# A two-layer fused block on one core: the sum of squares of the recurrence's heads as two rounded products, four key tiles later

## The chip, the cores and the metric

The kernel runs on one core of a Trainium2 chip. It is one program for a network of several layers. The metric is its device time in microseconds (us); the median of three runs of the kernel before is 1331.39 us.

## The reference

A sequence of 512 tokens with 1024 channels passes through three layers, in float32: a gated MLP with a spatial mix, a chunked attention, and a second block that has two branches. This case is about the first branch of the second block, a gated linear recurrence with 8 heads of 128 channels:

```python
def hgrn2_branch(hq, hf, hi, hz, lb, hg_norm_g):
    f = lb + (1.0 - lb) * jax.nn.sigmoid(hf.astype(jnp.float32))
    q = jax.nn.silu(hq.astype(jnp.float32)).reshape(B, S, HG_HEADS, HG_DIM)
    k = (1.0 - f).reshape(B, S, HG_HEADS, HG_DIM)
    v = hi.astype(jnp.float32).reshape(B, S, HG_HEADS, HG_DIM)
    log_f = jnp.log(f).reshape(B, S, HG_HEADS, HG_DIM)
    o = hgrn2_recurrence(q, k, v, log_f).astype(dt)
    o = rms_norm_2(o, hg_norm_g)
    o = o * jax.nn.silu(hz).reshape(B, S, HG_HEADS, HG_DIM)
    return o.reshape(B, S, HG_WIDTH)

def rms_norm_2(x, g):
    xf = x.astype(jnp.float32)
    y = xf * lax.rsqrt(jnp.mean(xf * xf, axis=-1, keepdims=True) + EPS)
    return (y * g.astype(jnp.float32)).astype(x.dtype)
```

`hgrn2_recurrence` computes S_t = diag(f_t) S_{t-1} + k_t v_t^T and o_t = S_t^T q_t in chunks. hq, hf, hi, hz and mz are slices of one projection of the normalised input. The mean of `rms_norm_2` over a head's 128 channels is what the change touches.

## The kernel before

Channels lie on the 128 partitions and the 512 tokens along the free dimension, so one head is a tile of 128 x 512. Weights come in slabs of 128 x 1024 (8 key tiles of 128 x 128). SyncE (SP) issues a slab's transfer into `raw`. ScalarE (ACT) rounds it to `whi` (line 1048, wherever its program says `cut()`), a type of fewer bits called fp32r. GpSimd (POOL) subtracts, and the rest is `wlo` (line 479). Every large product is then three products of rounded operands, hi x hi, hi x lo and lo x hi (lines 489 to 491, `mm3`), which TensorE (PE) takes faster than one of full float32. A ring of four slabs lies between ACT and PE.

Each engine has its own program, and works it in the order in which it is written; semaphores join the engines. A name such as `hoA.at("ln", u)` means ACT's step "ln" of head u. In the recurrence the rounds r = 0 to 8 overlap three heads: PE computes the projections of head r and the recurrence of head s = r - 1, and the normalisation of head u = r - 2 is finished.

PE's round is: slab hq of head r into bank 1, with pieces of the scores between its key tiles (`hg_scores`: the product of the squared output after key tile 2, the turned keys after 3, diagonal blocks after 4 and 5, cross blocks 0 and 1 after 6, 2 and 3 after 7); slab hf into bank 0, with the state's updates after key tiles 3 to 5 (`hg_updates`, which wait for the keys' low part, line 1830 on DVE); slab mz of head s into bank 7, after the masked copies (line 1840, step "far"); slab hz into bank 2, with the outputs (`hg_outputs`) into bank 3. The cross products of blocks 0 and 1 are written to bank 6, those of 2 and 3 to bank 7. Therefore `hg_cross` waits, at block 2, for the Silu of mz of head s - 1, which reads bank 7:

```python
                if t == 2 and s >= 1:
                    pe.wait_ge(mzA.sem, mzA.at("z", s - 1))
```

After round 7 the slabs dn 0 to 5 take the places of the next head's slabs.

ACT's round r is: `hg_root(u)` (the Square of the output in bank 3, line 1263; after PE's product the logarithm from bank 6, line 1265, and the exponential, line 1267); a slab's rounding; `hg_silu_z` of head s (line 1273, with a table load); `ml_silu_z(r - 2)` (the Silu of mz, line 1277); `hg_keys` (line 1283); a rounding; `hg_scores`; then the Silu of hq, the sigmoid and the logarithm of the forget gate and the decays of head r, and `hg_halves` (the rounded copies, lines 1325 to 1331).

VectorE (DVE) does in round r: `hg_finish(u)` (lines 1819 to 1826: norm, gate, and the two halves of y), `hg_stage(s)` (lines 1830 to 1851), `hg_project(r)` (lines 1856 to 1903; its last four subtractions are the low halves, line 1896 klo, 1898 kolo, 1900 qlo and 1903 qblo).

The product itself is `hg_square` on PE (line 762), in full float32: a matrix of ones with `ho[:, 0, :]` gives every partition the sum over the channels. It waits for the Square and for "far" of head u, and writes bank 6; cross block 0 of the next head waits for the logarithm, which reads that bank.

Of the kernel before, what the change touches and what calls it, by code (L numbers as in the profile page):

```python
# [22 lines left out]
F32 = mybir.dt.float32  # L23
F32R = mybir.dt.float32r
U32 = mybir.dt.uint32
ALU = mybir.AluOpType
ACT = mybir.ActivationFunctionType

P = 128
S = 512  # L30
# [8 lines left out]
HH = 8  # L39
# [105 lines left out]
def build(nc, xt, w, vecs, ws, bs, relx, consts, masks_hg, masks_ml, xs, rel_tab, tk, out):  # L145
    ctx = ExitStack()
    with ctx:
        def sb(name, shape, dt, where=ctx):
            return where.enter_context(nc.sbuf_tensor(name, shape, dt))
# [76 lines left out]
        with ExitStack() as scope:  # L226
            he = sb("he", [P, S], F32, scope)
            hf = sb("hf", [P, S], F32, scope)
            hk = sb("hk", [P, S], F32, scope)
            hb = sb("hb", [P, S], F32, scope)  # L230
            hd = sb("hd", [P, S], F32, scope)
            heb = sb("heb", [P, S], F32, scope)
            hen = sb("hen", [P, S], F32, scope)
            hq = sb("hq", [P, S], F32, scope)
            hx = sb("hx", [P, TT, 12], F32, scope)
            hfac = sb("hfac", [P, TT, 12], F32, scope)
            hqx = sb("hqx", [P, TT, HX], F32, scope)
            hqxs = [sb(n, [P, TT, HX], F32R, scope) for n in ("hqxhi", "hqxlo")]
            hqb = sb("hqb", [P, TT - 1, P], F32, scope)
            hqbs = [sb(n, [P, 2, TT - 1, P], F32R, scope) for n in ("hqbhi", "hqblo")]  # L240
            hks = [sb(n, [P, S], F32R, scope) for n in ("hkhi", "hklo")]
            hkos = [sb(n, [P, S], F32R, scope) for n in ("hkohi", "hkolo")]
            hkb = sb("hkb", [P, TT - 1, P], F32, scope)
            hkts = [sb(n, [P, TT - 1, P], F32R, scope) for n in ("hkthi", "hktlo")]
            hs = sb("hs", [P, S], F32, scope)
            hss = [sb(n, [P, S], F32R, scope) for n in ("hshi", "hslo")]
            hst = sb("hst", [P, TT - 1, P], F32, scope)
            hsts = [sb(n, [P, TT - 1, P], F32R, scope) for n in ("hsthi", "hstlo")]
            hz = sb("hz", [P, 2, S], F32, scope)
            ho = sb("ho", [P, 2, S], F32, scope)  # L250
            hm = sb("hm", [P, S + P + CROSS], F32, scope)
# [54 lines left out]
        def steps(name, names, rounds=1, prime=0):  # L306
            s = Steps(sem(name), names, rounds, prime)
            all_steps.append(s)
            return s
# [58 lines left out]
        htA = steps("ht_act", ["z", "kthi", "shi", "sthi"], HH)  # L368
        htV = steps("ht_dve", ["ktlo", "diag", "near", "mid", "far", "slo", "st1", "st2", "st3", "stlo"], HH)
        hoP = steps("ho_pe", ["ms"], HH)  # L370
        hoA = steps("ho_act", ["sq", "ln", "root"], HH)
        hoV = steps("ho_dve", ["norm", "y", "yhi", "ylo"], HH)
        mzA = steps("mz_act", ["z"], HH)
        hzV = steps("hz_dve", ["zero", "one0", "one1"])
        dnP = steps("dn_pe", ["tok", "wide"])
        dnA = steps("dn_act", numbered("sq", QL + KL) + ["kp", "root", "wide0", "wide1"] + numbered("hi", QL + KL))
        dnV = steps("dn_dve", ["q1", "q2", "k1"] + ["turn"] + numbered("cross", 4) + ["sum", "mean", "inv", "kplo", "diag"]
# [38 lines left out]

        def col(name, i=0):
            return vec[:, bass.ds(VEC[name] + i, 1)]

        def f32(ap):  # L420
            return ap.bitcast(F32)
# [62 lines left out]
        def _(pe):  # L484
# [261 lines left out]
            def hg_cross(s, t):  # L746
                if t == 0:
                    if s >= 1:
                        pe.wait_ge(htV.sem, htV.at("far", s - 1))
                        pe.wait_ge(hoA.sem, hoA.at("ln", s - 1))  # L750
                if t == 2 and s >= 1:
                    pe.wait_ge(mzA.sem, mzA.at("z", s - 1))
                cols = slice(t * P, (t + 1) * P)
                last = mm3(banks[:, 6 * S + t * 2 * P:6 * S + t * 2 * P + CROSS], [u[:, cols] for u in hkos],
                           [u[:, t, HC:HX] for u in hqxs], True, True)
                if t == TT - 1:
                    last.then_inc(htP.did("cross"), 1)

            def hg_square(u):
                pe.wait_ge(hoA.sem, hoA.at("sq", u))  # L760
                pe.wait_ge(htV.sem, htV.at("far", u))
                nc.tensor.matmul(bank[6], ones, ho[:, 0, :], start=True, stop=True).then_inc(hoP.did("ms"), 1)  # L762

            def hg_scores(r, k):
                s, u = r - 1, r - 2
                if k == 2 and u >= 0:
                    hg_square(u)
                if k == 3:
                    hg_keys(s)
                if k in (4, 5):  # L770
                    hg_diagonal(s, 2 * (k - 4))
                    hg_diagonal(s, 2 * (k - 4) + 1)
                if k in (6, 7):
                    hg_cross(s, 2 * (k - 6))
                    hg_cross(s, 2 * (k - 6) + 1)

            def hg_updates(s, k):
# [29 lines left out]
            for r in range(HH):  # L807
                s = r - 1
                scores, updates, outputs = (lambda k: hg_scores(r, k), lambda k: hg_updates(s, k),
                                            lambda k: hg_outputs(s, k))  # L810
                if s < 0:
                    scores = updates = outputs = None
                if r >= 1:
                    pe.wait_ge(hpA.sem, hpA.at("q", r - 1))
                if r == 1:
                    pe.wait_ge(hvV.sem, hvV.all())
                slab("hq", r, bank[1], h, between=scores, tiles=n2V if r == 0 else None)
                if r >= 1:
                    pe.wait_ge(hpA.sem, hpA.at("f", r - 1))
                slab("hf", r, bank[0], h, between=updates)  # L820
                if s >= 0:
                    pe.wait_ge(htV.sem, htV.at("far", s))
                    slab("mz", s, bank[7], h)
                if r == 0:
                    values(1)
                if r == 0:
                    pe.wait_ge(n2V.sem, n2V.all())
                if r >= 1:
                    pe.wait_ge(htA.sem, htA.at("z", s))
                slab("hz", r, bank[2], h, between=outputs)  # L830
# [2 lines left out]
            pe.wait_ge(hpA.sem, hpA.at("q", s))  # L833
            slab("dn", 0, bank[1], h, between=lambda k: hg_scores(HH, k))
            pe.wait_ge(hpA.sem, hpA.at("f", s))
            slab("dn", 1, bank[0], h, between=lambda k: hg_updates(s, k))
            pe.wait_ge(htV.sem, htV.at("far", s))
            slab("mz", s, bank[7], h)
# [191 lines left out]
        def _(act):  # L1030
# [228 lines left out]
            def hg_root(u):  # L1259
                if u >= 1:  # L1260
                    act.wait_ge(hoV.sem, hoV.at("ylo", u - 1))
                act.wait_ge(htP.sem, htP.at("o", u))
                nc.scalar.activation(ho[:, 0, :], bank[3], ACT.Square).then_inc(hoA.did("sq"), 1)
                act.wait_ge(hoP.sem, hoP.at("ms", u))
                nc.scalar.activation(ho[:, 1, :], bank[6], ACT.Ln, bias=eps, scale=1.0 / P).then_inc(hoA.did("ln"), 1)
                act.wait_ge(hoA.sem, hoA.at("ln", u))
                nc.scalar.activation(ho[:, 1, :], ho[:, 1, :], ACT.Exp, scale=-0.5).then_inc(hoA.did("root"), 1)

# [228 lines left out]
        def _(dve):  # L1497
# [316 lines left out]
            def spread(ap, shape):  # L1814
                return ap.to_broadcast([P, *shape])

            def hg_finish(u):
                dve.wait_ge(hoA.sem, hoA.at("root", u))
                V.scalar_tensor_tensor(ho[:, 0, :], bank[3], cols("hg_g", 1)[0], ho[:, 1, :], ALU.mult,
                                       ALU.mult).then_inc(hoV.did("norm"), 1)  # L1820
                dve.wait_ge(hoV.sem, hoV.at("norm", u))
                V.tensor_tensor(ho[:, 0, :], ho[:, 0, :], hz[:, u % 2, :], ALU.mult).then_inc(hoV.did("y"), 1)
                dve.wait_ge(hoV.sem, hoV.at("y", u))
                V.tensor_copy(yhi[:, u, :], ho[:, 0, :]).then_inc(hoV.did("yhi"), 1)
                dve.wait_ge(hoV.sem, hoV.at("yhi", u))
                V.tensor_tensor(ylo[:, u, :], ho[:, 0, :], f32(yhi[:, u, :]), ALU.subtract).then_inc(hoV.did("ylo"), 1)
# [27 lines left out]
            def hg_project(r):  # L1854
# [44 lines left out]
                dve.wait_ge(hpA.sem, hpA.at("qhi", r))  # L1899
                V.tensor_tensor(hqxs[1][:, :, :], hqx[:, :, :], f32(hqxs[0][:, :, :]),  # L1900
                                ALU.subtract).then_inc(hpV.did("qlo"), 1)
                dve.wait_ge(hpA.sem, hpA.at("qbhi", r))
                V.tensor_tensor(hqbs[1][:, r % 2, :, :], hqb[:, :, :], f32(hqbs[0][:, r % 2, :, :]),
                                ALU.subtract).then_inc(hpV.did("qblo"), 1)
# [1 line left out]
            V.memset(hs[:, :], 0.0).then_inc(hzV.did("zero"), 1)  # L1906
            V.memset(hfac[:, :, 0:1], 1.0).then_inc(hzV.did("one0"), 1)
            V.memset(hfac[:, :, 11:12], 1.0).then_inc(hzV.did("one1"), 1)
            dve.wait_ge(st_x, 16)
            dve.wait_ge(ld_hm, 16)  # L1910
            dve.wait_ge(hzV.sem, hzV.all())
# [300 lines left out]
```

## Time and profile before

| | |
|---|---|
| median of three runs | 1331.39 us (1330.42 to 1332.16) |
| the profiled execution | 1331.94 us |
| its span in the trace | 1330.0 us |
| mean granted clock of PE | 0.994 of full speed |
| PE busy | 1299.5 us |
| DVE, ACT, POOL busy | 730.7, 663.1, 495.9 us |

The page sums up one profiled execution. Times are us unless marked ns. "PEld" is PE's weight load, which overlaps the matmuls. The timeline's rows give the start, the duration, the engine, the line and the tiles; a bracket at the end holds the idle time before the instruction and what ended it. Matmuls are pipelined: the next one starts before the last has ended, so the distance between starts, not the duration, is what each takes from the stream. The product of ones has two records per head.

### The profile page before, as it was taken

What the parts mean: (1) busy time and instruction counts of PE and PEld (TensorE: products, weight loads), DVE (VectorE), ACT (ScalarE), POOL (GpSimd) and SP (SyncE); (2) the same over time, 40 slices, a digit from 0 to 9 for tenths busy, and PEclk for the clock granted to TensorE, in tenths of its full rate; (3) what the DMA queues carried; (4) which work ended last, traced back from release to release, by engine and by line L of the source; (5) the groups of instructions that cost most, each with busy time, mean ns of one, the idle gap of its engine ahead of it and who ended that gap; (6) DMA issues with size and microseconds to landing.
All of it is one profiled execution on the core that took longest, in us unless ns stands there. A gap on an engine that the chain in (4) does not pass through costs nothing.

```text
span 1330.0 us, 16592 instructions
## 1 busy us (share of the span) xinstructions
PE 1299.5 (98%) x6492; PEld 1086.2 (82%) x6492; DVE 730.7 (55%) x1290; ACT 663.1 (50%) x998; POOL 495.9 (37%) x206
## 2 busy tenths in 40 slices
PE   6999999999999999999999999999999999999997
PEld 4788888888887788888887888888878888888897
DVE  6473655643129256565766377676646556642454
ACT  4344454443335566666446566665536555552321
POOL 3453443344434332322336433333333233344520
PEclk9999999999999999999999999999999999999998
DMA  6543233234333232231243322222223222335411
GB/s 227 177 140 98 89 94 95 90 101 142 95 111 89 86 109 79 93 95 63 65 158 93 110 80 64 64 78 72 73 88 99 72 90 72 97 93 177 145 54 64
DMA packets 43309, 132.33 MB, mean 99 GB/s; under 512 B 7072, under 2 KB 11872, under 8 KB 42592
## 3 DMA queue, kind: packets, MB, share of 16 engines
q1 hardware_dynamic: 37856, 116.41, 28.1%
q10 hardware_dynamic: 5376, 14.87, 3.2%
q8 instruction: 51, 0.84, 0.3%
q14 instruction: 26, 0.21, 0.1%
HBM read 124.97 MB, written 10.49 MB: 102 GB/s over the span
## 4 chain that ended last, share of the span: by engine, by line
PE 80%; DVE 10%; ACT 6%; issue 2%; POOL 1%; DMA 0%; DVEq 0%; SPq 0%; ACTq 0%
PE banks L489 24%; PE banks L491 24%; PE banks L490 24%; PE banks L656 2%; DVE hd L1862 1%; PE banks L648 1%; PE banks L637 1%; DVE naccb L1767 1%; DVE ylo L1664 1%; ACT L1307 1%; ACT L1306 1%; PE banks L881 1%; PE banks L762 1%; DVE nfull L1660 1%; DVE hb L1859 1%
## 5 line engine op out<-in xcount | busy, mean ns | idle before, releaser
L479 POOL TENSOR_TENSOR wlo<-raw,whi 128x1024 fp32r<-128x1024 f32 (+2 forms) x198 | 486.2, 2457 | 761.2 <-ACT whi L1048 760.9
L489 PE MATMUL banks<-hhi,whi 128*128 128x512 f32 x752 | 304.7, 405 | 2.1 <-DVE hlo L1794 1.2
L1048 ACT ACTIVATE whi<-raw 128x1024 fp32r<-128x1024 f32 (+2 forms) x198 | 205.9, 1041 | 176.6 <-PE banks L491 104.5
L491 PE MATMUL banks<-hlo,whi 128*128 128x512 f32 x752 | 293.8, 391 | 0.0
L490 PE MATMUL banks<-hhi,wlo 128*128 128x512 f32 x752 | 293.4, 390 | 0.0
L489 PE MATMUL banks<-yhi,whi 128*128 128x512 f32 x448 | 176.6, 394 | 0.2 <-DVE ylo L1664 0.2
L491 PE MATMUL banks<-ylo,whi 128*128 128x512 f32 x448 | 174.7, 390 | 0.0
L490 PE MATMUL banks<-yhi,wlo 128*128 128x512 f32 x448 | 174.4, 389 | 0.0
L489 PEld LDWEIGHTS banks<-hhi,whi 128*128 128x128 f32 x752 | 141.6, 188 | 31.7 <-issue 2.8
L491 PEld LDWEIGHTS banks<-hlo,whi 128*128 128x128 f32 x752 | 141.1, 188 | 30.3
L490 PEld LDWEIGHTS banks<-hhi,wlo 128*128 128x128 f32 x752 | 141.7, 188 | 26.9 <-issue 2.2
L489 PE MATMUL banks<-whi,yhi 128*128 128x512 f32 x224 | 91.6, 409 | 15.3 <-DVE ylo L1523 12.3
L489 PEld LDWEIGHTS banks<-yhi,whi 128*128 128x128 f32 x448 | 84.1, 188 | 21.3 <-issue 3.0
L491 PEld LDWEIGHTS banks<-ylo,whi 128*128 128x128 f32 x448 | 84.1, 188 | 18.0
L490 PEld LDWEIGHTS banks<-yhi,wlo 128*128 128x128 f32 x448 | 84.2, 188 | 17.0
L490 PE MATMUL banks<-whi,ylo 128*128 128x512 f32 x224 | 89.4, 399 | 0.0
L491 PE MATMUL banks<-wlo,yhi 128*128 128x512 f32 x224 | 89.4, 399 | 0.0
L489 PEld LDWEIGHTS banks<-whi,yhi 128*128 128x128 f32 x224 | 43.5, 194 | 26.3 <-POOL wlo L479 15.7
L490 PEld LDWEIGHTS banks<-whi,ylo 128*128 128x128 f32 x224 | 43.6, 195 | 9.7 <-issue 0.7
L491 PEld LDWEIGHTS banks<-wlo,yhi 128*128 128x128 f32 x224 | 43.3, 193 | 9.4
L1610 DVE SCALAR_TENSOR_TENSOR mt<-banks,vec,bb 128x512 f32<-128x512 f32 x16 | 12.0, 751 | 68.3 <-PE banks L578 68.3
L1179 ACT ACTIVATE sc<-sc,sm 128x128 f32<-128x128 f32 (+1 forms) x64 | 35.1, 550 | 27.5 <-DVE sm L1722 27.5
(382 smaller groups left out, 2198.7 us busy)
## 6 DMA issues: line engine op xcount, KB each, us to landing
raw<-w SPq DMA_DIRECT2D x194, 512.0 KB, 3.6
rel_tab<-relx ACTq DMA_DIRECT2D x1, 4096.0 KB, 20.1
tab<-rel_tab SPq DMA_DIRECT2D x16, 224.0 KB, 3.5
x<-xt SPq DMA_DIRECT2D x4, 512.0 KB, 6.6
x<-xt ACTq DMA_DIRECT2D x1, 2048.0 KB, 9.4
x_kept<-x ACTq DMA_DIRECT2D x1, 2048.0 KB, 7.5
parts_kept<-mcg SPq DMA_DIRECT2D x8, 256.0 KB, 4.3
mgt<-parts_kept SPq DMA_DIRECT2D x8, 256.0 KB, 4.1
```

Source lines behind the costliest of these rows:

```text
L479: nc.gpsimd.tensor_tensor(lo[:, 0:width], raw[:, n % 2, 0:width], f32(hi[:, 0:width]), ALU.subtract).then_inc(lo_done, 1)
L489: nc.tensor.matmul(dst, a[0], b[0], start=first, stop=False)
L490: nc.tensor.matmul(dst, a[1], b[0], start=False, stop=False)
L491: return nc.tensor.matmul(dst, a[0], b[1], start=False, stop=last)
L637: done = nc.tensor.matmul(banks[:, c:c + QW[t]], a[rows, t * P:(t + 1) * P], b[rows, 0:QW[t]], start=first, stop=last)
L648: last = nc.tensor.transpose(banks[:, c:c + P], sc[:, q, of:of + P], ident)
L656: last = nc.tensor.matmul(bank[AO[i][q]][:, k * P:S], av[q][:, i, k, :], p[:, q, AK[q][k]:AK[q][k] + KW[k]], start=k == 0 and p is phi, st ...
L762: nc.tensor.matmul(bank[6], ones, ho[:, 0, :], start=True, stop=True).then_inc(hoP.did("ms"), 1)
L881: last = nc.tensor.transpose(bank[b][:, c:c + P], msc[:, QO[t] + k * P:QO[t] + (k + 1) * P], ident)
L1048: nc.scalar.activation(parts(slab)[0][:, 0:width], raw[:, n % 2, 0:width], ACT.Copy).then_inc(hi_done, 1)
L1179: e = nc.scalar.activation(row, row, ACT.Exp, bias=sm[:, q, 1, t:t + 1], accum_out=sm[:, q, 2, t:t + 1])
L1306: nc.scalar.activation(he[:, :], bank[0], ACT.Sigmoid).then_inc(hpA.did("f"), 1)
```

## The change

In the recurrence the product of ones with the squared output of head u becomes two products of rounded operands. ACT makes a rounded copy `hsqhi` of the square behind the Square, once DVE has read `hq` (whose place it shares); DVE subtracts it into `hsqlo` (which shares the place of `heb`), between qlo and qblo of the next head, or in `hg_finish` for the last head. A rounded copy of the ones, `hones`, is made once. PE issues the two products in key tile 6 of slab hq, after cross block 0, instead of after key tile 2. For heads 0 to 6 they are written to bank 0, which slab hf fills next, so slab hf waits for the logarithm; for the last head to bank 6, as before, and behind slab dn 3, as before. The wait of cross block 0 for the logarithm is gone.

```diff
+            hsqlo = sb("hsqlo", [P, S], F32R, scope)
+            hsqhi = sb("hsqhi", [P, S], F32R, scope)
+            hones = sb("hones", [P, P], F32R, scope)
...
+        def sum_bank(u):
+            return bank[0] if u < HH - 1 else bank[6]
...
                 if t == 0:
                     if s >= 1:
                         pe.wait_ge(htV.sem, htV.at("far", s - 1))
-                        pe.wait_ge(hoA.sem, hoA.at("ln", s - 1))
                 if t == 2 and s >= 1:
                     pe.wait_ge(mzA.sem, mzA.at("z", s - 1))
...
             def hg_square(u):
-                pe.wait_ge(hoA.sem, hoA.at("sq", u))
-                pe.wait_ge(htV.sem, htV.at("far", u))
-                nc.tensor.matmul(bank[6], ones, ho[:, 0, :], start=True, stop=True).then_inc(hoP.did("ms"), 1)
+                pe.wait_ge(hoV.sem, hoV.at("sqlo", u))
+                if u < HH - 1:
+                    pe.wait_ge(hpA.sem, hpA.at("f", u + 1))
+                else:
+                    pe.wait_ge(htV.sem, htV.at("far", u))
+                nc.tensor.matmul(sum_bank(u), hones[:, :], hsqhi[:, :], start=True, stop=False)
+                nc.tensor.matmul(sum_bank(u), hones[:, :], hsqlo[:, :], start=False, stop=True).then_inc(hoP.did("ms"), 1)
 
             def hg_scores(r, k):
                 s, u = r - 1, r - 2
-                if k == 2 and u >= 0:
-                    hg_square(u)
...
                 if k in (6, 7):
                     hg_cross(s, 2 * (k - 6))
+                    if k == 6 and u >= 0:
+                        hg_square(u)
                     hg_cross(s, 2 * (k - 6) + 1)
...
+                if r >= 2:
+                    pe.wait_ge(hoA.sem, hoA.at("ln", r - 2))
                 slab("hf", r, bank[0], h, between=updates)
...
+            pe.wait_ge(hoA.sem, hoA.at("ln", s - 1))
             slab("dn", 1, bank[0], h, between=lambda k: hg_updates(s, k))
...
                 nc.scalar.activation(ho[:, 0, :], bank[3], ACT.Square).then_inc(hoA.did("sq"), 1)
+                act.wait_ge(hoA.sem, hoA.at("sq", u))
+                act.wait_ge(hpV.sem, hpV.at("qin", min(u + 1, HH - 1)))
+                nc.scalar.activation(hsqhi[:, :], ho[:, 0, :], ACT.Copy).then_inc(hoA.did("sqhi"), 1)
                 act.wait_ge(hoP.sem, hoP.at("ms", u))
-                nc.scalar.activation(ho[:, 1, :], bank[6], ACT.Ln, bias=eps, scale=1.0 / P).then_inc(hoA.did("ln"), 1)
+                nc.scalar.activation(ho[:, 1, :], sum_bank(u), ACT.Ln, bias=eps, scale=1.0 / P).then_inc(hoA.did("ln"), 1)
...
+            def hg_square(u):
+                dve.wait_ge(hoA.sem, hoA.at("sqhi", u))
+                V.tensor_tensor(hsqlo[:, :], ho[:, 0, :], f32(hsqhi[:, :]), ALU.subtract).then_inc(hoV.did("sqlo"), 1)
...
             def hg_finish(u):
+                if u == HH - 1:
+                    hg_square(u)
...
+                if r >= 1:
+                    hg_square(r - 1)
                 dve.wait_ge(hpA.sem, hpA.at("qbhi", r))
...
+            V.tensor_copy(hones[:, :], ones).then_inc(hzV.did("ones"), 1)
```

## Rows read from the trace of the kernel before

**Rows 1.** The page, part 1: busy time, share, instructions.
```profile
PE 1299.5 (98%) x6492; PEld 1086.2 (82%) x6492; DVE 730.7 (55%) x1290; ACT 663.1 (50%) x998; POOL 495.9 (37%) x206
```

**Rows 2.** Windows view, 30 us of the recurrence; the columns stand in the row.
```profile
core 0: us, PE busy (x) PEld busy (x) DVE busy (x) ACT busy (x) POOL busy (x), PEclk, DMA share, GB/s
790.00:820.00 30.00, 29.85 (x159) 24.95 (x158) 20.59 (x36) 19.04 (x27) 10.87 (x4) 1.00 0.24 74
```

**Rows 3.** Waits from 720 to 1000 us: us in total, times, longest.
```profile
PEld banks L762 <- ACT ho L1263: 4.0, 7, 0.6
...
ACT ho L1265 <- PE banks L762: 12.9, 8, 4.4
```

**Rows 4.** Timeline, PE around the product of head 0: start us, us.
```profile
769.74 0.39 PE L491 MATMUL banks<-hlo,whi 128*128 128x512 f32 x1
...
770.26 0.30 PEld L762 LDWEIGHTS banks<-ho,cst 128*128 128x128 f32 x2 [0.55 <-ACT ho L1263]
770.26 1.12 PE L762 MATMUL banks<-ho,cst 128*128 128x512 f32 x2
...
771.45 0.39 PE L490 MATMUL banks<-hhi,wlo 128*128 128x512 f32 x1
...
771.68 0.39 PE L491 MATMUL banks<-hlo,whi 128*128 128x512 f32 x1
...
772.71 0.19 PEld L489 LDWEIGHTS banks<-hqxhi,hkhi 128*128 128x128 f32 x1
...
799.88 0.70 PE L762 MATMUL banks<-ho,cst 128*128 128x512 f32 x1 [0.15 <-ACT ho L1263]
```

**Rows 5.** Timeline, ACT from the Square to the Silu of mz.
```profile
769.63 0.58 ACT L1263 ACTIVATE ho<-banks 128x512 f32<-128x512 f32 x1
771.43 0.69 ACT L1265 ACTIVATE ho<-banks,cst 128x512 f32<-128x512 f32 x1 [1.22 <-PE banks L762]
...
772.68 1.04 ACT L1048 ACTIVATE whi<-raw 128x1024 fp32r<-128x1024 f32 x1
773.75 1.28 ACT L1273 ACT_TABLE_LOAD   x1
775.04 0.60 ACT L1273 ACTIVATE hz<-banks 128x512 f32<-128x512 f32 x1
775.53 0.59 ACT L1277 ACTIVATE mzg<-banks 128x512 f32<-128x512 f32 x1
```

**Rows 6.** Timeline, PE: cross block 1, end of key tile 7, cross block 2.
```profile
775.98 0.27 PE L489 MATMUL banks<-hqxhi,hkohi 128*128 128x192 f32 x1
...
776.80 0.39 PE L491 MATMUL banks<-hlo,whi 128*128 128x512 f32 x1
...
777.03 0.25 PE L489 MATMUL banks<-hqxhi,hkohi 128*128 128x192 f32 x1
```

**Rows 7.** Timeline, DVE: low halves, the keys' low part, the masked copies.
```profile
769.09 0.68 DVE L1896 TENSOR_TENSOR hklo<-hen,hkhi 128x512 fp32r<-128x512 f32 x1
...
770.29 1.08 DVE L1900 TENSOR_TENSOR hqxlo<-hqx,hqxhi 128x896 fp32r<-128x896 f32 x1
...
777.47 0.55 DVE L1830 TENSOR_TENSOR hktlo<-banks,hkthi 128x384 fp32r<-128x384 f32 x1
...
778.77 1.43 DVE L1840 COPY_PREDICATED hs<-hm,banks 128x384 f32<-128x384 uint32 x3
```

**Rows 8.** Timeline, PE: first state update, first matmul of slab mz.
```profile
780.45 0.22 PE L489 MATMUL banks<-yhi,hkthi 128*128 128x128 f32 x1
...
784.21 0.39 PE L489 MATMUL banks<-hhi,whi 128*128 128x512 f32 x1
```

**Rows 9.** Timeline and windows view around the longest later pause of PE.
```profile
45.19 0.77 PE L489 MATMUL banks<-whi,yhi 128*128 128x512 f32 x1 [3.00 <-POOL wlo L479]
...
48.72 0.39 PE L491 MATMUL banks<-wlo,yhi 128*128 128x512 f32 x1
...
46.00:47.00 1.00, 1.00 (x3) 0.75 (x3) 0.00 (x0) 0.00 (x0) 1.00 (x1) 0.50 0.95 152
```

More of the change, by code:

```diff
@@ L231, in build @@
             hd = sb("hd", [P, S], F32, scope)
-            heb = sb("heb", [P, S], F32, scope)
+            with ExitStack() as place:
+                heb = sb("heb", [P, S], F32, place)
+            hsqlo = sb("hsqlo", [P, S], F32R, scope)
             hen = sb("hen", [P, S], F32, scope)
-            hq = sb("hq", [P, S], F32, scope)
+            with ExitStack() as place:
+                hq = sb("hq", [P, S], F32, place)
+            hsqhi = sb("hsqhi", [P, S], F32R, scope)
+            hones = sb("hones", [P, P], F32R, scope)
             hx = sb("hx", [P, TT, 12], F32, scope)
@@ L370, in build @@
         hoP = steps("ho_pe", ["ms"], HH)
-        hoA = steps("ho_act", ["sq", "ln", "root"], HH)
-        hoV = steps("ho_dve", ["norm", "y", "yhi", "ylo"], HH)
+        hoA = steps("ho_act", ["sq", "sqhi", "ln", "root"], HH)
+        hoV = steps("ho_dve", ["sqlo", "norm", "y", "yhi", "ylo"], HH)
         mzA = steps("mz_act", ["z"], HH)
-        hzV = steps("hz_dve", ["zero", "one0", "one1"])
+        hzV = steps("hz_dve", ["zero", "one0", "one1", "ones"])
         dnP = steps("dn_pe", ["tok", "wide"])
```

## The prediction

> **What bounds the kernel now.** I read the page first: TensorE (PE) has work in 98% of the span [rows 1]. In a stretch of 30 us in the middle of the recurrence it is busy 29.85 us, at a granted clock of 1.00, while VectorE (DVE) is busy 20.59, ScalarE (ACT) 19.04 and GpSimd (POOL) 10.87 us [rows 2]. So what is added to PE's stream, or makes it stand still, lengthens the kernel one for one, and work on the other engines is free until PE waits for it. The waits of this stretch come next: PE waits for the squared output seven times, 4.0 us in sum, at the place that the change touches, and ACT waits 12.9 us for the product that follows [rows 3]. ACT's idle time costs nothing by itself. I then laid one round of the timelines side by side (the product of head 0 at 770.26 us) and asked of every instruction behind the moved product who waits for it. The rounds repeat: the same instructions stand 29.6 us later each time (line 762 again at 799.88) [rows 4].
>
> **The product itself.** Before it, line 491 begins at 769.74 us; a pair of 512-column products follows each other by 0.23 us (771.45 to 771.68). Without the product line 490 of key tile 3 would have begun at 769.74 + 2 x 0.23 = 770.20; it begins at 771.45 [rows 4]. So wait and float32 product together cost PE 1.25 us: 770.26 - 769.97 = 0.29 of waiting for the Square, 0.96 of product. The two rounded products are of the same form as the stream around them and cost 2 x 0.23 = 0.46 us. The Square's output is 2.7 us old or more at the new place, so the first wait goes. Gain on PE: 1.25 - 0.46 = 0.79 us a round, seven times. For the last head the product stays where it is, behind slab dn 3, and only its kind changes: 0.96 - 0.46 = 0.5 us gained, once.
>
> **The added instructions.** ACT gets one rounding copy a round, of 128 x 512 like the Square of 0.58 us, between Square and logarithm [rows 5]; ACT waits there for the product anyhow. It is done by about 770.9 (769.63 + 2 x 0.6). DVE gets one subtraction, 0.68 us by the row of the same form; it stands behind the subtraction of line 1900, which ends at 771.37, so it is ready at about 772.1 [rows 7]. The new product comes at 774.7 (below): 2.6 us of cover, so neither costs anything. Line 1903, now 0.7 us later, is wanted only in slab hz, over 20 us later. The copy of the ones is made once, before the loop, 128 columns wide, beside a PE that has other work: nothing. The wait for the forget gate's sigmoid before bank 0 is written concerns an instruction of the round before: nothing. PE runs 1.25 us earlier in key tiles 3 to 6, and its weight load for the diagonal products moves from 772.71 to 771.46 [rows 4], against line 1900's end at 771.37 [rows 7]: 0.04 us are left after the 0.05 that a signal takes. I put this at zero, at most 0.1 us a round.
>
> **What the move delays.** This is the term that decides. The product was issued after key tile 2 and is now issued in key tile 6, between the cross products of block 0 and block 1. That place is 775.98 us before [rows 6], so 775.98 - 1.25 = 774.73 in the changed kernel. The second of the two begins at 774.96, lasts 0.39 like its neighbours [rows 4], and ends at 775.35; ACT starts 0.05 us later, as it did behind the old one (770.26 + 1.12 = 771.38, then 771.43) [rows 4, 5]. The logarithm so begins at 775.40 instead of 771.43: 3.97 us later.
>
> ACT works its list strictly in order, and behind the logarithm stand, without an idle moment between them: the exponential, a slab's rounding (line 1048), a table load of 1.28 us, the Silu of hz and the Silu of mz, which ends at 775.53 + 0.59 = 776.12 [rows 5]. All of them move by 3.97 us: the Silu of mz ends at 780.09. PE waits for exactly this one: hg_cross of block 2, in key tile 7, waits for mzA "z" of the head before, because blocks 2 and 3 are written to bank 7, which that Silu reads. Before the change the wait was met, since the matmul of block 2 began at 777.03 [rows 6] and the Silu had ended 0.9 us earlier. Now the square that is issued in key tile 6 releases a chain of 4.7 us on ACT, and the wait at its end comes some 1.1 us of PE work later. With 0.05 us for the signal and a weight load of 0.19 the matmul of block 2 begins at 780.33. Without the wait it would begin at 777.03 - 0.79 = 776.24. PE stands still for 4.1 us, and the round ends 780.33 - 777.03 = 3.30 us later than before. Heads 0 to 6 have this round, the last head has not: 7 x 3.30 = 23.1 us.
>
> What is late next? DVE's chain hangs on the exponential too: the low part of the keys (line 1830) ends at 778.02 and would end at 781.99 [rows 7]; the update that needs it stood at 780.45 and stands at 783.75 after the stall [rows 8]. The masked copies end at 780.20, so at 784.17 [rows 7], for slab mz, which moves from 784.21 to 787.51 [rows 8]. Both are covered by the stall itself. The new wait of slab hf for the logarithm (ending at 776.1) is covered too. The slabs' rounding moves with ACT, but its results are wanted a slab or more later, and POOL is busy a third of the time. SP's transfers start from POOL's end and move by the same 4 us, beneath that lead.
>
> **The clock.** PE's last matmul before the stall (line 491, 776.80 [rows 6]) would start at 776.01 and end at 776.40, so PE is idle for 3.9 us. The trace has one comparable pause: 3.00 us idle before 45.19. Behind it the granted clock is 0.50, the level of 1.2 GHz, and the eight matmuls from 45.19 to 48.72 took 3.53 us instead of 8 x 0.23 = 1.84: 1.7 us lost [rows 9]. So each of the seven stalls can cost between nothing and 1.7 us on top. I take 1.2: the pause is longer than the one that cost 1.7, but when the clock falls while PE still stands, a part of the slow time runs out unused. That makes 7 x 1.2 = 8.4 us, between 0 and 12.
>
> The Trainium skill, "TensorE: Matmul & The Clock Gate", section "Why this matters for your kernels", warns of idle gaps between matmul bursts, which bring the clock back to half rate. By that rule each stall pays the term, by its absence the stalls cost 23.1 us alone; the pause of 3.00 us in this trace agrees with the page.
>
> **Sum.** Profiled span 1330.0 + 23.1 - 0.5 + 8.4 = 1361.0 us. The profiled execution took 1331.94, 1.94 around its span, and stands 0.55 over the median of 1331.39. So 1361.0 + 1.94 - 0.55 = 1362.4 us.
>
> **Rivals.**
> - No loss of clock: the stall is as computed, and PE returns at full clock. 1362.4 - 8.4 = 1354.0. For it: the trace holds one such pause, in another stage and beside other work. Against it: rows 9, a shorter pause that did cost. Chance 0.14.
> - Full loss of clock in every round, 12.0 us: 1366.0. For it: the pause is longer than that of rows 9. Chance 0.13.
> - The Silu of mz isn't what PE meets, and the keys' low part is: the update would stand at 780.45 - 0.79 = 779.66 and find its operand at 781.99, a stall of 2.3 us, 1.5 net, a pause short of that of rows 9. 7 x 1.5 - 0.5 = 10.0: 1341.4. Against it: the order of ACT's list and the wait in hg_cross are both in the code. Chance 0.04.
> - The other side: the chain on ACT ends in time. The mechanism is the slack at block 2 in key tile 7: the wait costs nothing as long as logarithm to Silu of mz fits into the 0.9 us that PE needs from the product's end to that matmul, and it decides from there. Then only the gain of PE remains: 7 x 0.79 + 0.5 = 6.0, 1325.4. The chain is 4.69 us long in rows 5, table load and slab's rounding included, and would have to be four fifths shorter. Chance 0.04 for this result, 0.01 for a chain so nearly hidden that gain and stall cancel.
>
> **How the numbers follow.** The forecast has 0.64. The range 1353 to 1368 takes in the first two rivals and the bounds of the clock term, and leaves out those with 0.09. A difference under 0.2% (2.7 us) couldn't be told from no change. Faster: 0.04; same: 0.01; slower: 0.95, the sum of the forecast, both clock cases and the keys.
>
> **What would show it.** In the profile of the changed kernel: two fp32r matmuls on the square between 192-column cross products, seven times, and no wait of PE on line 1263's output in them; seven waits of PE's weight load on the Silu of mz, about 3.9 us each, some 27 in sum, a wait that isn't there before; ACT's wait for the product near 4.5 us a round instead of 1.2; heads 32.9 us or more apart instead of 29.6; a granted clock under 1.00 in stretches of the recurrence; no wait on the keys' low part or on the masked copies. The prediction is wrong if PE doesn't wait at block 2, or waits without the clock falling (then by 8 us), or if the two rounded products cost far from 0.46 us.

## The result and the profile after

The changed kernel takes 1368.28 us (median of four runs, 1366.86 to 1369.89) against 1331.78 us for the kernel before in the same comparison: a ratio of 1.0273, 95% interval 1.0257 to 1.0290. It is slower by 36.5 us; forecast were 31.0, and the time lies 0.3 us above the upper end of the range.

The profiled execution took 1368.03 us, its span is 1366.1 us and the mean granted clock 0.982 of full speed (before: 1330.0 us and 0.994). The page's part 1 and the head of part 2 of the changed kernel, beside [rows 1]:

```profile
span 1366.1 us, 16610 instructions
PE 1310.0 (96%) x6492; PEld 1097.2 (80%) x6492; DVE 737.3 (54%) x1299; ACT 667.4 (49%) x1006; POOL 494.4 (36%) x206
...
PE   6999999999999999999999888888899999999997
```

PE is 10.5 us longer busy, although the changed products take less of its stream (part of its matmuls last longer, see below), and it stands still for longer as well: seven of the forty slices, those of the recurrence, fall from 9 to 8. The waits view of 720 to 1036 us says on whom (engine and line that waited, who ended it, us in sum, times, longest), beside [rows 3]:

```profile
PE banks L497 <- ACT mzg L1294: 26.3, 7, 3.8
...
PEld banks L497 <- ACT mzg L1294: 29.3, 7, 4.2
...
ACT ho L1282 <- PE banks L773: 35.0, 8, 4.5
```

Line 497 is the first of the three products of `mm3` in the new file, 1294 the Silu of mz, 773 the second rounded product, 1282 the logarithm. No wait of PE on the Square is left, and there is no other new one. The timeline of the first such round, beside [rows 5, 6]:

```profile
768.91 0.58 ACT L1277 ACTIVATE ho<-banks 128x512 f32<-128x512 f32 x1
...
773.98 0.42 PE L772 MATMUL banks<-hsqhi,hones 128*128 128x512 f32 x1
774.24 0.39 PE L773 MATMUL banks<-hsqlo,hones 128*128 128x512 f32 x1
...
774.67 0.69 ACT L1282 ACTIVATE ho<-banks,cst 128x512 f32<-128x512 f32 x1 [4.51 <-PE banks L773]
775.39 0.63 ACT L1284 ACTIVATE ho<-ho 128x512 f32<-128x512 f32 x1
775.93 1.04 ACT L1062 ACTIVATE whi<-raw 128x1024 fp32r<-128x1024 f32 x1
776.99 1.28 ACT L1290 ACT_TABLE_LOAD   x1
778.28 0.60 ACT L1290 ACTIVATE hz<-banks 128x512 f32<-128x512 f32 x1
778.77 0.59 ACT L1294 ACTIVATE mzg<-banks 128x512 f32<-128x512 f32 x1
...
775.27 0.40 PE L499 MATMUL banks<-hlo,whi 128*128 128x512 f32 x1
779.42 0.53 PE L497 MATMUL banks<-hqxhi,hkohi 128*128 128x192 f32 x1 [3.75 <-ACT mzg L1294]
...
781.72 0.63 PE L499 MATMUL banks<-hlo,whi 128*128 128x512 f32 x1
...
784.69 0.40 PE L497 MATMUL banks<-hhi,whi 128*128 128x512 f32 x1
```

The rows show the Square (768.91), the chain without a gap from the product to the Silu of mz (774.24 to 779.36), PE's cross block 2 starting 0.06 us behind it, and what follows: a matmul of 512 columns lasts 0.63 us instead of 0.39 until 784.7. The windows view gives the clock in these stretches (last columns: granted clock, DMA share, GB/s):

```profile
776.00:779.00 3.00, 0.00 (x0) 0.00 (x0) 2.88 (x3) 2.97 (x5) 1.96 (x1) 0.80 0.00 0
779.00:780.00 1.00, 0.58 (x3) 0.58 (x3) 1.00 (x1) 1.00 (x3) 0.73 (x1) 0.50 0.00 0
780.00:784.00 4.00, 4.00 (x13) 3.32 (x13) 3.17 (x7) 1.27 (x3) 2.38 (x1) 0.50 0.49 137
785.00:790.00 5.00, 5.00 (x28) 4.29 (x27) 0.99 (x3) 0.59 (x1) 0.00 (x0) 1.00 0.19 78
```

In this round the clock falls to half, 1.2 GHz, while PE stands still, and is back at 2.4 GHz at 784.7, when PE has worked for 5.2 us. Not every round is like this. Read in windows of 0.2 us, the clock is at half from 777.8 to 784.7, 815.4 to 818.8, 849.5 to 852.9, 883.6 to 887.1, 917.8 to 921.2, 951.9 to 958.7 and 989.5 to 992.9 us, while PE starts again at 779.42, 814.68, 849.08, 883.52, 917.95, 952.25 and 988.09. In four of the seven rounds it therefore falls only after PE has started again, and in the first and the sixth it stays low for 6.8 us instead of 3.4. The third and the sixth round:

```profile
849.10:849.50 0.40, 0.40 (x3) 0.40 (x4) 0.40 (x1) 0.40 (x2) 0.30 (x1) 1.00 0.00 0
849.60:852.80 3.20, 3.20 (x11) 2.62 (x11) 3.00 (x7) 0.76 (x1) 2.36 (x1) 0.50 0.48 164
...
952.00:958.60 6.60, 6.34 (x18) 5.28 (x19) 4.71 (x8) 2.64 (x5) 2.95 (x2) 0.50 0.51 144
```

The sum of the seven rounds can be read from the Squares on ACT. They lie 35.25, 34.42, 34.43, 34.43, 34.31, 35.83 and 32.88 us apart; before they lay 29.61, 29.60, 29.62, 29.61, 29.67, 29.65 and 28.10 us apart. That is 35.7 us in all. Block 2 comes 779.42 - 768.91 = 10.51 us behind the Square and came 777.03 - 769.63 = 7.40 behind it: 3.11 us a round (the other rounds agree within 0.02), 21.8 in sum, are the wait, less PE's gain. The rest, 2.53, 1.71, 1.70, 1.71, 1.53, 3.07 and 1.67 us, 13.9 in sum, is the half clock. The intervals above give nearly the same: half of the low time in which PE works is 2.6, 1.7, 1.7, 1.7, 1.6, 3.2 and 1.7 us, 14.3 in sum.

### The profile page after: what moved, and what is told of

The parts are those of the page before. It is cut to its first block, busy times and chain, and to the rows that moved or that the text cites. A ratio compares the mean times of both kernels' runs of the same rounds, so it can differ in the third digit from the quotient of the medians.

```text
span 1366.1 us, 16610 instructions
## 1 busy us (share of the span) xinstructions
PE 1310.0 (96%) x6492; PEld 1097.2 (80%) x6492; DVE 737.3 (54%) x1299; ACT 667.4 (49%) x1006; POOL 494.4 (36%) x206
## 4 chain that ended last, share of the span: by engine, by line
PE 86%; DVE 6%; ACT 4%; issue 2%; POOL 1%; DMA 1%; DVEq 0%; SPq 0%; ACTq 0%
PE banks L497 27%; PE banks L499 26%; PE banks L498 26%; PE banks L664 1%; PE banks L656 1%; PE banks L645 1%; DVE naccb L1784 1%; DVE ylo L1681 1%; ACT whi L1062 1%; DMA raw<-w 1%; ACT L1290 1%; PE banks L895 1%; DVE nfull L1677 1%; PE banks L586 1%; DVE hlo L1811 0%
## 5 line engine op out<-in xcount | busy, mean ns | idle before, releaser
L498 PE MATMUL banks<-hhi,wlo 128*128 128x512 f32 x752 | 298.1, 396 | 0.0
L499 PE MATMUL banks<-hlo,whi 128*128 128x512 f32 x752 | 297.9, 396 | 0.0
L497 PEld LDWEIGHTS banks<-hhi,whi 128*128 128x128 f32 x752 | 144.8, 193 | 31.3 <-DVE hlo L1811 2.8
L499 PEld LDWEIGHTS banks<-hlo,whi 128*128 128x128 f32 x752 | 144.2, 192 | 31.4
L498 PEld LDWEIGHTS banks<-hhi,wlo 128*128 128x128 f32 x752 | 144.9, 193 | 26.3 <-issue 0.2
## 6 DMA issues: line engine op xcount, KB each, us to landing
rel_tab<-relx ACTq DMA_DIRECT2D x1, 4096.0 KB, 20.4
```

The source lines that it names most:

```text
L497: nc.tensor.matmul(dst, a[0], b[0], start=first, stop=False)
L498: nc.tensor.matmul(dst, a[1], b[0], start=False, stop=False)
L499: return nc.tensor.matmul(dst, a[0], b[1], start=False, stop=last)
```

## The experiments

Each was measured in three rounds with the kernel before on the same chip. The first three take the changed kernel's mechanism apart, the next two its halves, the last five look for an order in which the change pays.

**Another place: after key tile 4.** 

```diff
-                    if k == 6 and u >= 0:
+                    if k == 4 and u >= 0:
                         hg_square(u)
```

(The call stands behind the second diagonal block of that tile.)

> The changed kernel with the two products after key tile 4 instead of 6, 2.4 us earlier. Theory: the chain to the Silu of mz starts 2.4 us earlier, so a round loses 3.1 - 2.4 = 0.7 us net and PE's pause is 1.4 us; 7 x 0.7 - 0.5 = 4.4 us over the kernel before, 1336 us, and no fall of the clock. If the clock falls in such a pause too: 1350. Rival (the place doesn't matter, the two products or the bank do): 1368.

Measured: 1338.49 us, ratio 1.0049 (1.0034 to 1.0064), 6.0 us over the kernel before by the medians. The waits and the mean clock (0.993):

```profile
PE banks L497 <- ACT mzg L1294: 9.5, 7, 1.4
...
PEld banks L497 <- ACT mzg L1294: 12.6, 7, 1.8
```

The same wait, 2.4 us shorter seven times, as the place is 2.4 us earlier. None of the seven pauses was followed by slow matmuls; the one slow stretch near the recurrence stands behind it (999.8 to 1006.6). So place and chain set the loss, not the products or the bank; and of the 30 us that this kernel gains on the changed one only 17 (7 x 2.4) are waiting.

**A shorter chain: the slab's rounding behind the Silus.**

```diff
                     hg_root(u)
-                cut()
                 if s >= 0:
                     hg_silu_z(s)
                 if r >= 2:
                     ml_silu_z(r - 2)
+                cut()
```

> The changed kernel with the slab's rounding on ScalarE (1.04 us) behind the Silu of mz instead of ahead of the Silus. Theory: the rounding is a link of the chain from the product to block 2; without it the pause is 1.0 us shorter, 2.7 us, and a round costs 3.1 - 1.0 = 2.1 us of waiting. Without a fall of the clock 7 x 2.1 - 0.5 = 14 us over the kernel before, 1346 us; with the same loss by the clock as in the changed kernel (2.0 us a round) 1360. Rival (the chain isn't what PE waits for): 1368.

Measured: 1357.78 us, ratio 1.0184 (1.0161 to 1.0207). PE's pauses on the Silu of mz are 2.8 us each instead of 3.75: the rounding of 1.04 us is a link of the chain. Slow matmuls follow in five of the seven rounds of the profiled execution (mean clock 0.986; one of the four executions had 0.990 and took 1353.04). In the profiled execution a round without them lasts 31.87 us (from one pause's start to the next, 877.01 to 908.88), the rounds with them 33.4 or 33.5: 1.6 us a fall.

**The pause filled.** (The cross blocks' old calls in key tiles 6 and 7 go.)

```diff
+                if k == 6 and u >= 0:
+                    hg_square(u)
+                if k == 7:
+                    if u >= 0:
+                        pe.wait_ge(htV.sem, htV.at("far", u))
+                        for _ in range(15):
+                            nc.tensor.matmul(bank[6], hones[:, :], hhi[:, 0, :], start=True, stop=True)
+                    for t in range(TT):
+                        hg_cross(s, t)
```

> The changed kernel with 15 idle-filling matmuls of 512 columns a round (into bank 6, overwritten at once) before the cross products, which all stand in key tile 7; the product of ones stands 0.3 us earlier. PE is busy in what was its pause, the chain on ScalarE is as long as before. Theory (the pause costs twice, once as waiting and once through the clock): the waiting part stays, 7 x 2.8 - 0.5 = 19 us over the kernel before, but the clock doesn't fall: 1351 us, granted clock 0.99. Rival (the clock falls for another reason, or the lost time isn't the clock's): 1365 us.

Measured: 1352.91 us, ratio 1.0158 (1.0143 to 1.0174), mean clock 0.992. In this kernel the 15 matmuls stand where the pause was, and the work behind them runs at full clock. The chain still sets the time: the Silu of mz ends at 779.26, and cross block 2 starts at 779.32.

```profile
775.05 3.65 PE L789 MATMUL banks<-hhi,hones 128*128 128x512 f32 x15
778.54 0.25 PE L497 MATMUL banks<-hqxhi,hkohi 128*128 128x192 f32 x1
...
780.32 0.40 PE L498 MATMUL banks<-hhi,wlo 128*128 128x512 f32 x1
```

The windows view of 30 us from 770, first of this kernel, then of the changed one:

```profile
770.00:800.00 30.00, 30.00 (x161) 25.59 (x160) 18.31 (x32) 16.74 (x24) 10.84 (x4) 1.00 0.24 71
```

```profile
770.00:800.00 30.00, 26.25 (x130) 22.12 (x128) 15.47 (x24) 14.95 (x21) 10.76 (x4) 0.89 0.18 53
```

This kernel is 20.4 us over the kernel before by the medians of its comparison and does 15 idle-filling products more per round; the changed one, which only waits at that place, is 36.5 over it. The two kernels are 15.4 us apart. Some 1.7 of that is the chain, since the products stand earlier here: a head takes 32.48 us from block 2 to block 2, against 29.61 + 3.11 = 32.72 in the changed kernel without the half clock. The other 13.7 us are what the clock costs, close to the 13.9 us read from the rounds.

**The halves of the change.** First the move without the kind: in the changed kernel `hg_square` issues the float32 product again, still in key tile 6 and bank 0.

```diff
-                nc.tensor.matmul(sum_bank(u), hones[:, :], hsqhi[:, :], start=True, stop=False)
-                nc.tensor.matmul(sum_bank(u), hones[:, :], hsqlo[:, :], start=False, stop=True).then_inc(hoP.did("ms"), 1)
+                nc.tensor.matmul(sum_bank(u), ones, ho[:, 0, :], start=True, stop=True).then_inc(hoP.did("ms"), 1)
```

> The move without the change of kind: the product is again one in float32, at the new place and in bank 0; copy and subtraction are still made. Theory: the product ends 0.5 us later than the two rounded ones, and everything behind it too; 8 x 0.5 = 4 us over the changed kernel, 1372 us, so the loss belongs to the move. Rival (the rounded kind or its operands cost the time): nearer to 1332 than to 1368.

Measured: 1374.57 us (1370.14 to 1374.64), ratio 1.0309 (1.0287 to 1.0331). The expected 1372 lies inside the scatter of its four executions. Its seven pauses are 3.76 us each, and slow matmuls follow all seven. The move alone brings the whole loss.

Then the kind without the move: the call of `hg_square(u)` goes back to `k == 2`.

> The change of kind without the move: the two rounded products after key tile 2, where the float32 one stood, still in bank 0. Theory: PE waits there for VectorE's subtraction, about 2.0 us a round instead of 0.3, and then spends 0.5 instead of 0.96: 7 x (2.0 + 0.46 - 1.25) - 0.5 = 8 us over the kernel before, 1340 us, no pause at block 2 and no fall of the clock. Rival (the kind costs as much as the place): above 1350.

Measured: 1343.53 us, ratio 1.0081 (1.0062 to 1.0101), 11.4 us over the kernel before.

```profile
PE banks L772 <- DVE hsqlo L1836: 13.3, 7, 1.9
...
PEld banks L772 <- DVE hsqlo L1836: 16.3, 7, 2.3
```

PE waits 2.3 us a round for the subtraction, 0.3 more than expected, and slow matmuls follow two of the seven pauses of 1.9 us (from 772.58 and from 868.48 us). The longer waits (2.3 us in seven rounds) and the two slow stretches (1.7 us each) come to 5.7 us, and the profiled execution (1345.81, the slowest of four) is 5.7 us over the expected 8; the other three have a higher mean clock and are faster. So neither half pays by itself: the rounded products come too early at the old place, and at the new one they are too late for ACT.

**ACT in another order.** In the changed kernel, `hg_root` is cut in two: Square and copy stay, logarithm and exponential (`hg_root_end`, with its table load asked for ahead) follow the Silus and the keys.

```diff
                     hg_root(u)
-                cut()
                 if s >= 0:
                     hg_silu_z(s)
                 if r >= 2:
                     ml_silu_z(r - 2)
                 if s >= 0:
                     hg_keys(s)
+                if u >= 0:
+                    hg_root_end(u)
+                cut()
+                if s >= 0:
                     cut()
                     hg_scores(s)
```

> The changed kernel with another order on ScalarE: the Silus of hz and mz and the rounded copy of the keys come between the copy of the square and the logarithm, so cross block 2 no longer hangs on the product. Theory (the wait at block 2 is the whole stall): PE doesn't wait for the Silu of mz; the keys' low part is late next, because VectorE still finishes head u first. It ends 1.6 us after its old place, so 7 x 1.6 - 0.5 = 10.7 us over the kernel before, 1342.5 us, plus up to 14 us if the clock falls in a pause of 2.3 us too. Rival (the pause comes from the product itself, its bank 0 or its operands): the pause stays in key tile 7 and the time near 1368.

Measured: 1372.12 us, ratio 1.0298 (1.0281 to 1.0315). PE doesn't wait for the Silu of mz in this kernel any more; it waits for the keys' low part, as named, but for twice as long:

```profile
776.36 0.75 DVE L1850 SCALAR_TENSOR_TENSOR ho<-banks,vec,ho 128x512 f32<-128x512 f32 x1 [4.33 <-ACT ho L1288]
777.14 0.69 DVE L1853 TENSOR_TENSOR ho<-ho,hz 128x512 f32<-128x512 f32 x1
777.87 2.49 DVE L1855 CAST yhi<-ho 128x512 fp32r<-128x512 f32 x1
780.40 2.71 DVE L1857 TENSOR_TENSOR ylo<-ho,yhi 128x512 fp32r<-128x512 f32 x1
783.03 0.55 DVE L1861 TENSOR_TENSOR hktlo<-banks,hkthi 128x384 fp32r<-128x384 f32 x1
...
777.35 5.21 POOL L487 TENSOR_TENSOR wlo<-raw,whi 128x1024 fp32r<-128x1024 f32 x2 [13.02 <-ACT whi L1062]
...
783.63 0.48 PE L497 MATMUL banks<-yhi,hkthi 128*128 128x128 f32 x1 [4.22 <-DVE hktlo L1861]
```

The subtraction that makes the low half of y took 2.71 us, and 0.69 in the changed kernel. My edit had put two slabs' roundings back to back, so GpSimd worked from 777.35 to 782.56, beside both of these steps. The next kernel tests whether that is the cause.

**The two roundings apart** (`cut()`, `hg_scores(s)`, `cut()` instead of `cut()`, `cut()`, `hg_scores(s)`).

> As a_silu_first, but of the two slabs that ScalarE rounded back to back behind the exponential, the second is rounded after the scores' copy, later. Theory (in a_silu_first GpSimd's two subtractions ran through both of VectorE's steps that lie before the keys' low part and slowed each to 2.5 to 2.7 us): the low half of y takes 0.7 us again, the keys' low part is done 2.0 us earlier, PE's pause is 2.2 instead of 4.2 us, and the time is 1343 us plus the clock's loss in some of the rounds, about 1346. Rival (the pause has another cause than GpSimd's timing): 1372.

Measured: 1352.63 us, ratio 1.0157 (1.0142 to 1.0172). The low half of y takes 0.69 us again and PE's pause is 2.2 us:

```profile
775.91 2.73 POOL L487 TENSOR_TENSOR wlo<-raw,whi 128x1024 fp32r<-128x1024 f32 x1 [13.01 <-ACT whi L1062]
...
776.43 2.49 DVE L1855 CAST yhi<-ho 128x512 fp32r<-128x512 f32 x1
778.96 0.69 DVE L1857 TENSOR_TENSOR ylo<-ho,yhi 128x512 fp32r<-128x512 f32 x1
```

GpSimd is done at 778.64, just before the low half starts. So its timing was the cause of the 2.0 us. The time is 6.6 us over what I expected. Part of that has names in the trace: slow matmuls in four rounds, and two waits of 1.4 us in weight loads for the low half of the queries (DVE's hqxlo). Every round between two pauses holds the one or the other, so I leave the split open.

**Both orders.** ACT as in the kernel with the Silus first, and DVE does `hg_stage` up to the masked copies before `hg_finish`:

```diff
+                if r >= 1:
+                    hg_stage(r - 1)
                 if r >= 2:
                     hg_finish(r - 2)
                 if r >= 1:
-                    hg_stage(r - 1)
+                    hg_stage_end(r - 1)
                 hg_project(r)
```

> As a_silu_first, and VectorE does the keys' low part and the masked copies of head s before it finishes head u. Theory: both chains that the late product delays are out of PE's way; only PE's gain is left, 7 x 0.79 + 0.5 = 6.0 us, so 1325.8 us and a clock near that of the kernel before. Rival (two table loads more a round on ScalarE, or the later finish of head u, make a new wait): 1332 or more, with a wait of PE on a line of ScalarE or VectorE that stands in neither kernel.

Measured: 1326.23 us, ratio 0.9957 (0.9942 to 0.9972), mean clock 0.994. Both chains are out of PE's way. In the recurrence one wait is left, most of it in weight loads (PE itself stood for 0.7 us, once):

```profile
PEld banks L497 <- DVE hqxlo L1933: 2.0, 5, 1.2
```

With the float32 product in this order:

> As b_both_orders, with the product again in float32 at the new place. Both orders keep PE free of the late product's chains, so this shows what the change of kind is worth alone: theory 0.96 - 0.46 = 0.5 us for each of eight products, 4 us over b_both_orders, 1330 us. Rival (the kind is worth nothing, all of the gain comes from the wait that went): 1326.

Measured: 1328.57 us, ratio 0.9974 (0.9964 to 0.9983). That is 2.3 us over the median of the kernel with rounded products, 0.3 a product; but the two were measured in different comparisons, and against its own kernel before each gains 3.1 and 6.3 us, which makes 3.2, or 0.4 a product. The trace gives 0.40: from the last product of cross block 0 to the second of block 1 there are 1.08 us (773.47 to 774.55), and 0.68 in the changed kernel (773.88 to 774.56). The gain of the kind is real and small.

And with the roundings apart:

> As b_both_orders, with the two slabs' roundings apart as in h_casts_apart. Theory: VectorE's slowed steps aren't on PE's path in b_both_orders, so nothing changes: 1326 us. Rival (they are): a gain of 1 us or more.

Measured: 1325.36 us, ratio 0.9951 (0.9935 to 0.9968). The medians lie 0.9 us apart and the intervals overlap: not told apart from the kernel with both orders. These two are the fastest of the study, 0.4 to 0.5% under the kernel before. With only the two orders added, the change brings what its PE work was worth.

## Why the prediction was wrong

Direction, place and the wait were right. The time fell 0.3 us outside the range and 5.9 us above the forecast because one term of the sum, the loss by the clock, was mis-sized.

- **PE's gain.** Forecast 0.79 us a round, 0.5 for the last head. Cross block 1 starts 774.47 - 768.91 = 5.56 us behind the Square and started 775.98 - 769.63 = 6.35 behind it: 0.79. The last head shows 0.41 us (line 499 at 1015.49 to line 498 at 1016.41, 0.92 us, against 980.51 to 981.84, 1.33, before). Seven rounds and the last together: 6.3 us by each of the two kernels in which hardly anything else is late (1326.23 against 1332.49, 1325.36 against 1331.68), against 6.0.
- **The added instructions.** Nothing, as forecast, in the changed kernel. The margin of 0.04 us that I put at zero shows up where PE gets there sooner: 2.0 us of waiting in weight loads, in five rounds of the kernel with both orders.
- **What the move delays.** Forecast: logarithm 3.97 us later, the Silu of mz and then block 2 behind it, 3.30 us a round. Measured 3.11. The chain came out as computed: the Silu of mz ends 10.45 us behind the Square, forecast 10.46. The difference is the weight load of 0.19 us, which I had put ahead of block 2; in the trace it and the matmul start together, 0.06 us behind the Silu. 21.8 instead of 23.1 us. The experiments on place, chain length and order each moved the wait as this step says.
- **What is late next.** Right for the changed kernel: no wait on the keys' low part. The kernel with the Silus first shows that it was really next in line, and that my price for it, made with the durations of [rows 7], held only as long as GpSimd's work fell where it fell before.
- **The clock: the step that failed.** I took 1.2 us a pause, between 0 and 1.7, on the ground that a part of the slow time runs out unused when the clock falls while PE still stands. Measured are 1.5 to 3.1 us, 2.0 on average, 13.9 in sum instead of 8.4, and over the 12 that I had called the bound. Two things were wrong in it. First, the discount: in four of the seven rounds the clock fell only after PE had started again, and no slow time ran out unused; in the fifth and sixth 0.2 and 0.3 us did, and only in the first 1.6. Second, the bound: [rows 9] was one event, and I read it as the most that a fall can cost, but in the first and sixth round the clock stayed low for 6.8 us, twice as long as in the others and in [rows 9]. The very pause of [rows 9] shows it too. In the profile of the changed kernel it is as long (3.02 us), and the fourteen matmuls behind it took 6.03 us instead of 3.22, a loss of 2.8 us instead of 1.7:

```profile
44.90 0.79 PE L497 MATMUL banks<-whi,yhi 128*128 128x512 f32 x1 [3.02 <-POOL wlo L487]
...
50.93 0.40 PE L499 MATMUL banks<-wlo,yhi 128*128 128x512 f32 x1
```

  In the twelve profiles the clock was low for 3.4 us behind this pause eight times, and for 6.8 us four times. Why it is the one or the other, no run here shows. The kernel with the filled pause shows that the term is the clock's: with nearly the same chain and no pause it goes. The page "TensorE: Matmul & The Clock Gate" of the Trainium skill, section "Why this matters for your kernels", which warns of such idle gaps, is borne out in all seven rounds.
- **Behind the recurrence.** A pause that both kernels have, 1.3 us on line 934 (before: 920), was followed in the changed kernel by one more slow stretch, 1030.35 to 1033.42 us, and not in the kernel before. Between the last Square and the end lie 355.64 us instead of 354.51: 1.1 us, or 1.5 with the 0.4 that the last head gained, that no step of the prediction held. So the same pause can cost something in one execution and nothing in another.

3.11 x 7 - 0.4 + 13.9 gives 35.3 us; with the stretch behind the recurrence, some 1.5, and a start of the recurrence that was 0.7 us earlier than in the profile before (which has a slow stretch more, 687.0 to 690.4, and a shorter one at 45.3), this makes the 36.1 us by which the spans differ.

## What to carry to other kernels

When an instruction is moved later in a busy engine's stream, follow what it releases on the other engines to the end of their in-order lists: the cost came from a Silu that stands four instructions behind the logarithm of the product and has nothing to do with it, and whose bank the busy engine needed a microsecond later. A pause of TensorE of some microseconds is to be priced with the slow clock behind it, from several pauses, and with one such event as a sample, not as a bound. The remedy was to put the late product's consumers at the end of both lists, not to move the product back.

## What the runs showed of the hardware

The pauses of PE in the recurrence, seven per kernel, and after how many of them matmuls ran at half clock: 1.4 us, none (place after key tile 4); 1.9 us, two (rounded products early); 2.2 us, four (roundings apart); 2.8 us, five (rounding behind the Silus); 3.75 us, seven (changed kernel); 3.76 us, seven (float32 moved); 4.2 us, seven (Silus first). A fall of the clock cost 1.5 to 3.1 us in the changed kernel. Each count is of one profiled execution, and the mean clock shows that others of the same kernel had fewer (1353.04 us at 0.990 against 1358.31 at 0.986 for the rounding behind the Silus).

In the recurrence the share rises with the length of the pause. Behind it the length tells less. There sixteen products of one column take 1.95 us (line 934 in most kernels). With a pause of 1.3 us ahead of them, the clock fell during or behind them in six of seven profiles; with a pause of at most 0.5 us ahead, still in two of five. The kernel with both orders is one of these:

```profile
986.36 1.95 PE L934 MATMUL banks<-cst,dsq 128*128 128x1 f32 x16
...
989.32 0.63 PE L497 MATMUL banks<-hhi,whi 128*128 128x512 f32 x1
```

PE is counted as busy there, so the idle time alone doesn't say whether the clock will fall.

Some of VectorE's steps from SBUF (the on-chip memory of the tiles) to SBUF stretch while GpSimd subtracts a slab: the rounded copy of 128 x 512 takes 2.5 us beside it, and 0.43 us in the last head, where GpSimd is idle; the subtraction of the same size 2.71 us beside it and 0.69 otherwise. It matters which starts first. The product with the gate took 0.69 us in the kernel with the Silus first, where it began 0.2 us ahead of GpSimd's subtraction, and 1.55 us with both orders, where it began inside one. And where VectorE's steps follow each other without a gap, as from 721.4 to 727.4 us in the changed kernel, they keep 0.69 us, and GpSimd's subtraction takes 6.90 us instead of 2.4. The masked copies, which read PSUM (the banks that PE writes), kept their time beside it (1.41 us for three).
